# Two attentions in a diffusion trunk: a unit's transpose moved one unit back, scores of the differential heads read from 64 partitions

## The reference, cut to what matters

```python
def _attend(q, k, v, q2=None, k2=None, lam=None):
    scale = d ** -0.5
    def probs(qb, kk):
        s = jnp.einsum("bqhd,bkhd->bhqk", qb, kk) * scale
        return jax.nn.softmax(s, axis=-1)
    def one(qbs):
        p = probs(qbs[0], k)
        if q2 is not None:
            p = p - lam * probs(qbs[1], k2)
        return jnp.einsum("bhqk,bkhe->bqhe", p, v)

# B) latent attention: 8 heads, q and k of 96 channels, v of 64
# C) differential attention: 4 heads, q and k hold two maps of 64 channels each, v of 128
o_d = _attend(q_d[..., 0, :], k_all[..., 0, :], v_all, q_d[..., 1, :], k_all[..., 1, :], lam)
```

## Time and profile before

| | |
|---|---|
| three runs, median (lowest to highest) | 2794.98 us (2786.76 to 2797.15) |
| the profiled execution, own time | 2793.52 us |
| its span | 2791.7 us |
| TensorE matmul busy | 2615.9 us, 94% of the span |
| VectorE busy | 1334.8 us, 48% |
| ScalarE busy | 676.0 us, 24% |
| GpSimd busy | 1329.9 us, 48% |
| chain that ended last, TensorE's share | 82% |
| chain that ended last, VectorE's share | 10% |

### The profile page before, as it was taken

How to read it: one execution, slowest core, us unless ns; L and a number is a source line. 1 busy time by engine, 2 the same in 40 slices (tenths; PEclk the granted TensorE clock), 3 DMA queues, 4 the chain that set the end, 5 groups by cost and what they waited for, 6 DMA issues and landing times.

```text
span 2791.7 us, 41528 instructions
## 1 busy us (share of the span) xinstructions
PE 2615.9 (94%) x17328; PEld 2412.8 (86%) x17328; DVE 1334.8 (48%) x1693; ACT 676.0 (24%) x1202; POOL 1329.9 (48%) x604
## 2 busy tenths in 40 slices
PE   4999989999999799999979999899999988999997
PEld 3879986777999799999968799668789988999997
DVE  5434255777225644253644422649742266253353
ACT  2252235215311211010122423351343112010011
POOL 2524540340666466666644255205235655666663
PEclk8989999999999899999989999999999998999999
DMA  6201214430222122222211022242112211222221
GB/s 246 68 16 52 69 63 181 172 123 7 70 76 69 47 75 76 76 76 76 70 52 53 16 74 71 91 179 72 38 31 76 74 63 54 76 76 76 71 73 61
DMA packets 62555, 215.33 MB, mean 77 GB/s; under 512 B 6688, under 2 KB 11168, under 8 KB 62112
## 3 DMA queue, kind: packets, MB, share of 16 engines
q1 hardware_dynamic: 56448, 203.97, 21.6%
q10 hardware_dynamic: 5920, 8.70, 0.9%
HBM read 208.15 MB, written 4.49 MB: 76 GB/s over the span
## 4 chain that ended last, share of the span: by engine, by line
PE 82%; DVE 10%; ACT 2%; DVEq 2%; issue 1%; ACTq 1%; SPq 1%; DMA 1%
PE big L451 21%; PE big L455 21%; PE big L454 21%; PE big L606 4%; PE last_two L637 2%; PE two L620 2%; PE last_two L533 1%; PE big L474 1%; DVE cols L1342 1%; PE big L477 1%; PE two L751 1%; PE big L478 1%; PE last_two L751 1%; DVE ff_lo L1299 1%; DVE sq L1687 1%
## 5 line engine op out<-in xcount | busy, mean ns | idle before, releaser
L420 POOL TENSOR_TENSOR w_hi<-raw,cst 128x1024 fp32r<-128x1024 f32 x288 | 556.9, 1934 | 1335.2 <-PE big L451 1218.7
L451 PE MATMUL big<-act_hi,w_hi 128*128 128x320 f32 x2784 | 877.9, 315 | 43.9 <-DVE act_lo L1462 23.3
L454 PE MATMUL big<-act_lo,w_hi 128*128 128x320 f32 x2784 | 869.1, 312 | 0.0
L455 PE MATMUL big<-act_hi,w_lo 128*128 128x320 f32 x2784 | 868.8, 312 | 0.0
L423 POOL TENSOR_TENSOR w_lo<-raw,w_hi 128x1024 fp32r<-128x1024 f32 x288 | 742.3, 2577 | 41.0
L451 PEld LDWEIGHTS big<-act_hi,w_hi 128*128 128x128 f32 x2784 | 530.7, 191 | 61.1 <-issue 45.6
L454 PEld LDWEIGHTS big<-act_lo,w_hi 128*128 128x128 f32 x2784 | 531.1, 191 | 0.9
L455 PEld LDWEIGHTS big<-act_hi,w_lo 128*128 128x128 f32 x2784 | 530.6, 191 | 0.0
L451 PE MATMUL big<-ff_hi,w_hi 128*128 128x320 f32 x1024 | 317.6, 310 | 4.8 <-DVE ff_lo L1299 4.8
L455 PE MATMUL big<-ff_hi,w_lo 128*128 128x320 f32 x1024 | 316.4, 309 | 0.0
L454 PE MATMUL big<-ff_lo,w_hi 128*128 128x320 f32 x1024 | 316.4, 309 | 0.0
(11 more groups left out here) (295 smaller groups left out, 3491.5 us busy)
## 6 DMA issues: line engine op xcount, KB each, us to landing
raw<-in_w SPq DMA_DIRECT2D x368, 512.0 KB, 3.5
first_mod<-in_first SPq DMA_DIRECT2D x16, 512.0 KB, 19.0
x<-in_x ACTq DMA_DIRECT2D x1, 2560.0 KB, 12.9
out_y<-x SPq DMA_DIRECT2D x8, 320.0 KB, 2.3
cst<-in_const ACTq DMA_DIRECT2D x1, 1664.0 KB, 19.2
small<-in_small ACTq DMA_DIRECT2D x2, 437.0 KB, 9.1
out_C<-c_new ACTq DMA_DIRECT2D x2, 258.0 KB
v_d<-in_past ACTq DMA_DIRECT2D x2, 256.0 KB, 3.0
```

The source lines that it names most:

```text
L420: nc.gpsimd.tensor_tensor(w_hi[:, to, :], raw[:, slot, :], ones[:, 0:1].to_broadcast([P, BLK]), ALU.mult)
L451: first = mm(ps, wh, ah, start=k == 0, stop=False)
L454: mm(ps, wh, al, start=False, stop=False)
L455: last = mm(ps, wl, ah, start=False, stop=k == nk - 1)
```

## The change

- On TensorE, turn `i` now holds scores(i+1), turn(i-2), values(i-3); on ScalarE copyT(i-2); on VectorE the outputs come one turn later. The loops are one turn longer.
- There are four sets of probability tiles instead of three (the fourth set of `da` is `sq`, that of `ma` is `rs`) and four sets of columns for maxima and sums.
- In `da` the scores of map `m` read `q_d` and `k_d` at partitions 64m to 64m+63, and contract over 64 partitions. `q_map`, its clearing, `lay_out` and the semaphore `q_map_ready` are gone.
- The modulation beside `ma` moves one turn back in each of its steps: multiplications in turns 5 to 8 of each ten, the row kept in turn 9, turned and added in turn 10.

```diff
-            return prob[:, maps * (i % 3) + m, :] if i % 3 < 2 else (t1, rs)[m]
+            if i % 4 < 2:
+                return prob[:, maps * (i % 4) + m, :]
+            if maps == 1:
+                return (t1, rs)[i % 4 - 2]
+            return (t1, rs)[m] if i % 4 == 2 else sq[:, m, :]
...
-                    if p < 4 and 4 <= at < 8:
-                        if at == 4:
+                    if p < 4 and 5 <= at < 9:
+                        if at == 5:
...
-                    if p < 4 and at == 9:
-                        mod_turn(l, q, one[1][:, 256:512])
+                    if i >= 10 and at == 0:
+                        mod_turn(l, q - 1, one[1][:, 256:512])
...
-                    if maps == 2 and t == 0:
-                        pe.wait_ge(q_map_ready, l * H_D + h + 1)
...
-                for i in range(-1, n + 2):
+                for i in range(-1, n + 3):
                     if i + 1 < n:
                         scores(i + 1)
                     if beside and 0 <= i:
                         beside(i)
-                    if 0 <= i - 1 < n:
-                        turn(i - 1)
-                    if 0 <= i - 2 and (i - 2) % side == side - 1:
-                        if beside and i % 10 == 1:
-                            pe.wait_ge(mod_kept, l * MOD_CHUNKS + 3 + (i - 11) // 10)
-                        values((i - 2) // side)
+                    if 0 <= i - 2 < n:
+                        turn(i - 2)
+                    if 0 <= i - 3 and (i - 3) % side == side - 1:
+                        if beside and i % 10 == 2:
+                            pe.wait_ge(mod_kept, l * MOD_CHUNKS + 3 + (i - 12) // 10)
+                        values((i - 3) // side)
...
-                attend(l, "da", 2, 1, 40, 4, lambda h, m: q_map[h % 2][:, m, :], lambda h, m: k_d[:, h, :],
+                attend(l, "da", 2, 1, 40, 4, lambda h, m: q_d[64 * m:64 * m + 64, h, :],
+                       lambda h, m: k_d[64 * m:64 * m + 64, h, :],
...
-                    if i >= 3:
-                        act.wait_ge(pT_ready, l * 60 + unit0 + i - 2)
+                    if i >= 4:
+                        act.wait_ge(pT_ready, l * 60 + unit0 + i - 3)
...
-                for i in range(-1, n + 1):
-                    if i >= 1 and maps == 1:
-                        copyT(i - 1)
+                for i in range(-1, n + 2):
+                    if i >= 2 and maps == 1:
+                        copyT(i - 2)
                     if i + 1 < n:
                         exps(i + 1)
-                    if i >= 1 and maps == 2:
-                        copyT(i - 1)
+                    if i >= 2 and maps == 2:
+                        copyT(i - 2)
...
-                    if i % 10 == 8:
+                    if i % 10 == 9 and i < 40:
                         keep_row(l, 2 + i // 10, one[1][:, 256:512])
...
-                        if maps == 2 and t == LATE and h + 2 < heads:
-                            lay_out(h + 2)
                     if 0 <= i < n:
                         normalise(i)
-                    if i >= side + 2 and i % side == 0:
-                        outputs((i - side - 2) // side)
+                    if i >= side + 3 and (i - 1) % side == 0:
+                        outputs((i - side - 3) // side)
...
-                for tile in q_map:
-                    for m in range(2):
-                        other = 64 * (1 - m)
-                        v.memset(tile[other:other + 64, m, :], 0.0)
...
-                lay_out(0)
-                lay_out(1)
```

More of the change, by code:

```diff
@@ L219, in trunk @@
         qm, km = at("qm", [P, 2, T], A0), at("km", [P, 2, T], A0 + 5120)
-        q_map = [stage, sq]
         vm = at("vm", [P, 5, H_M, DV_1], A0 + 10240)
@@ L282, in trunk @@
         lam_tmp = cols[:, 9:12]
-        neg_max, row_sum = cols[:, 12:16], cols[:, 16:20]
+        neg_max, row_sum = cols[:, 12:20], cols[:, 20:28]
         raw_loaded = [sem(f"raw_loaded{i}") for i in range(RAW)]
@@ L294, in trunk @@
         cond_done = sem("cond_done")
-        q_map_ready = sem("q_map_ready")
         gather_done, small_sum = sem("gather_done"), sem("small_sum")
@@ L554, in hook @@
                                 pe.wait_ge(o_copied, l * 16 + 2 * p)
-                        for k in (2 * at - 8, 2 * at - 7):
+                        for k in (2 * at - 10, 2 * at - 9):
                             mod_block(l, KD * q + k, one[1][:, 256:512])
-                    if p < 4 and at == 9:
-                        mod_turn(l, q, one[1][:, 256:512])
+                    if i >= 10 and at == 0:
+                        mod_turn(l, q - 1, one[1][:, 256:512])
                 return hook
@@ L950, in exps @@
                         ps, b, _ = buf(use)
-                        col = 2 * (i % 2) + m
+                        col = 2 * (i % 4) + m
                         act.wait_ge(maxed, l * 80 + exp0 + maps * i + m + 1)
@@ L1329, in merge, with attend @@
                         behind(m)
-            def attend(l, name, maps, side, unit0, set0, heads, prob, exp0, out, lay_out=None, beside=None):
+            def attend(l, name, maps, side, unit0, set0, heads, prob, exp0, out, beside=None):
                 units = attention_units(heads, side)
@@ L1347, in normalise @@
                     n = CTX if t == LATE else T
-                    c0 = 2 * (i % 2)
+                    c0 = 2 * (i % 4)
                     dve.wait_ge(exped, l * 80 + exp0 + maps * (i + 1))
@@ L1371, in attend @@
                 n = len(units)
-                for i in range(-1, n + 3):
+                for i in range(-1, n + 4):
                     if i + 1 < n:
                         maxes(i + 1)
-                        h, t = units[i + 1]
-                        if maps == 2 and t == LATE and h + 2 < heads:
-                            lay_out(h + 2)
                     if 0 <= i < n:
                         normalise(i)
-                    if i >= side + 2 and i % side == 0:
-                        outputs((i - side - 2) // side)
+                    if i >= side + 3 and (i - 1) % side == 0:
+                        outputs((i - side - 3) // side)
                     if beside and i >= 0:
@@ L1431, in hook @@
                 def hook(i):
-                    if i % 10 == 9 and i < 40:
-                        q = 2 + i // 10
+                    if i % 10 == 0 and 10 <= i <= 40:
+                        q = 1 + i // 10
                         keep_mod(l, q, q, one[1][:, 256:512])
@@ L1671, in _ @@
                 dve.drain().then_inc(v_copied, 1)
-                attend(l, "ma", 1, 2, 0, 0, H_A, prob_a, 0, o_a, None, mods_beside(l))
+                attend(l, "ma", 1, 2, 0, 0, H_A, prob_a, 0, o_a, mods_beside(l))
                 for k in range(4):
@@ L1694, in _ @@
                         keep_mod(l + 1, 0, FIRST_CHUNKS[0], one[1][:, 0:256])
-                for tile in q_map:
-                    for m in range(2):
-                        other = 64 * (1 - m)
-                        v.memset(tile[other:other + 64, m, :], 0.0)
-                def lay_out(h):
-                    for m in range(2):
-                        r = slice(64 * m, 64 * m + 64)
-                        v.tensor_copy(q_map[h % 2][r, m, :], q_d[r, h, :])
-                    dve.drain().then_inc(q_map_ready, 1)
-                lay_out(0)
-                lay_out(1)
                 if l + 1 < DEPTH:
                     keep_mod(l + 1, 1, FIRST_CHUNKS[1], one[1][:, 0:256])
-                attend(l, "da", 2, 1, 40, 4, H_D, prob_d, 40, q_d, lay_out)
+                attend(l, "da", 2, 1, 40, 4, H_D, prob_d, 40, q_d)
                 for h in range(H_D):
```

## The result

The changed kernel takes **2809.7 us** (median of 7 runs, 2805.9 to 2815.3) against 2796.4 us (2786.8 to 2800.8) of the kernel before in the same session: ratio 1.0055, 95% interval 1.0036 to 1.0073. It is slower by about 13 us. The forecast was 2790 us and the range ended at 2804; both the sign and the range were wrong.

The account below looks back on a forecast made before the run. TensorE, busy 94% of the span, was taken as the bound, so its idle time and work count. Differential attention -2.1 us per layer twice, latent 0: -4 us from 2793.5 to 2789.5, stated as 2790 us; range 2775 to 2804.

Parts of the forecast that it names:

- The clearing and laying out: Differential attention: removing them gains nothing, being hidden by projections before it and gap-free scores within, except where VectorE is the bound.
- 64 partitions: Differential scores: a full unit takes 1.6 us by partial overlap of the maps, against 2.16; bounds 1.08 and 2.16.
- The prediction's own sign against it: Differential attention, full unit: scores over 2.1 us or under 1.3 would show the forecast wrong.
- The changes of mode: TensorE, differential attention: two changes between 64 and 128 partitions per unit, 0.2 us each; bounds zero and 0.2.
- A head: Differential attention: one head takes 17.5 us against 18.3, still waiting before the short unit's second map and the transposes after.
- the faster rival: Differential scores: both maps fully beside each other, mode changes free; -8 us per layer, about 2777 us; chance 0.10.
- The ends, first part: Start of the differential attention: the first five units take 16.3 us against 17.1.
- the rival on the clock: Differential attention: clock falls to half, two slow starts and one slow head cost +20 us; 2810 us; chance 0.07.
- The ends, last part: End of the differential attention: the last head, with the loop's extra turn, takes 22.1 us against 21.85.
- Both steps on the waits: Latent attention, per pair of heads: probabilities wait goes (-0.6 us), turned row's wait grows to 1.2 (+0.4); sum 0.
- The clause on the refill: Latent attention: modulation blocks read one unit later delay their slots' refill by about 2.5 us, costing nothing through GpSimd.
- The other rival: Differential scores: no overlap, 2.16 us per unit, mode changes paid; +3.3 us per layer, 2800 us; chance 0.18.

Follow-up runs that it names:

- scores128b: The change, but with 128-partition differential scores and q_map back, clearing and layouts in their old place; ratio 1.0022 to the kernel before.
- warm: The change plus unread filler multiplications before the first differential scores and after each of the first four units' scores; ratio 1.0025 to the kernel before.
- da_deep_warm: Kernel before with 64-partition scores, fillers and the deeper order in the differential attention alone; ratio 0.9993 to the kernel before.
- ma_deep_warm: Kernel before with 64-partition scores, fillers and the deeper order in the latent attention alone; 2791.5 us, ratio 0.9986 to the kernel before.
- only64_warm2: Repetition of only64_warm, the same kernel in another session; ratio 0.9976 to the kernel before.
- only64_warm: Kernel before with 64-partition differential scores in the old order, plus fillers at the start and after three units; ratio 0.9982 to the kernel before.

## Why the prediction was wrong

**The clearing and laying out:** nothing ahead of the attention, as said. In scores128b, which has both back, the stage's first scores come after the same 1.9 us of idle time as in the change, behind ScalarE's copy. What the layouts within the attention cost, no run shows apart.

**64 partitions:** the step gave 1.6 us for a full unit's scores. The traces have 1.28 with the change of mode. The eight records start in pairs 0.01 us apart, the pairs 0.27 us apart but for the first step and the step to the transposes, which take 0.1 more each. That is the lower bound of 1.08 and 0.2 for the change, both maps wholly beside each other although both multiplications of map 0 stand ahead of map 1's. The prediction's own sign against it, scores under 1.3, had come. The scores reach this only where both PSUM buffers are free. The Trainium skill (TensorEngine Tiling (Array Packing), Theoretical Speedup), held at arm's length in the prediction for want of such a row, had this right.

**The changes of mode** came to 0.4 us in a unit, as taken: 0.2 in the scores, 0.1 ahead of them (values 1.23 us, 677.80 to 679.03, against 1.12) and 0.07 in the transposes behind (0.61 against 0.54). The Trainium skill (TensorEngine Tiling (Array Packing), Key Properties) says that changing the tiling mode drains TensorE; these rows show what it cost here.

**A head:** 17.7 against 17.5, by the expected pattern of waits. Faster scores didn't shorten it further, because then the exponential that frees the second buffer is late. This also answers the faster rival: its overlap came, its time did not.

**The ends, first part: this is the first step that failed.** The sum had 16.3 us for the first five units at full clock (three ways round and the piece behind; "four" in its words is a slip); they took 21.4. The way round was right, 3.15 us for the first unit. What failed was the weight of the rival on the clock. I gave it 0.07, because the same start ran at full clock in layer 1 of before. But there TensorE works for 2.16 us of each 3.15. Here it works for 1.35, less even than the 1.6 of my own rival. That start was not the same. And layer 2 of before, whose stretches I called alike, had begun at half clock (0.57 in 1981.9 to 1985.9) and taken 77.4 us, not 75.5: the fall was there to be read, and only its length was new.

The rival's price per way round (1.07) was near the measured 1.18, and its time, 2810 us, is the measured one, partly by luck: no head ran at half clock for more than its first 1 to 2 us, and the latent part, which it left at zero, supplied the difference. The Trainium skill (TensorE: Matmul & The Clock Gate, The HAM clock gate) has the clock follow how busy TensorE was recently; the trace agrees. The experiment on it is warm: filling the idle time with work nobody needs makes the stage 4.7 us shorter. The sign set for this, a granted clock under 0.9 in the first layer's stage, had come with 0.85.

**The ends, last part: the second.** 22.1 us were forecast for the last head, 24.1 measured (679.03 to 703.09) and 23.3 in layer 2. From the short unit's first map on, the sum has 8.35 us and the traces 10.0 and 9.4; the 0.6 between the layers goes with the short drop of the clock in layer 1, and the rest with the copies that the transposes wait for. I had added up TensorE's work there and left no wait in it.

So the differential stage of 73.4 forecast came to 81.3: +5.1 at the start, +0.8 over two heads (the first took 18.1 us, the second 17.7), +2.0 at the end.

**The latent attention: the third.** Both steps on the waits were right in sign and near in size (1.04 us before the turned row, forecast 1.2). The clause on the refill was not: it asked only whether GpSimd, which takes the same places later, would wait, and not whether the modulation's own multiplications would. Their next blocks land in the places they have just released, and the move left 0.9 us less from release to use. This cost 2.9 and 4.5 us in the profile where nothing was forecast.

**The sum.** Differential +5.8 and +3.8, latent +3.7 and +4.8 in the profiles; of the 13 us between the medians about 8 are the clock (change against warm). What the deeper order costs lies between da_deep_warm, ma_deep_warm and only64_warm2: 4.4 and 2.8 us in the medians, where the intervals leave 4 to 5 us either way; what shows both costs is the stage lengths, not the time.

The kernel warm, which has both, is 13 us over only64_warm, of which its four stages show 7. In the profiles most of the rest lies where nothing was edited, between the first layer's differential and the second layer's latent attention: TensorE's 6719 instructions there take 1088.8 us in warm and 1082.5 in only64_warm, and in the 200 us in which they part, up to and in the second layer's mLSTM, the granted clock is 0.89 against 0.93. That stretch took 1085.3 to 1089.0 us in the six kernels with the deeper order in both attentions and 1082.4 to 1082.8 in the others, but 1088.3 in the profile of before. So it may be the change's doing or not; the runs leave it open.

**The other rival,** no overlap at 2800 us, was wrong in its reason: the scores ran side by side.

## What to carry to other kernels

When a change makes TensorE's work shorter in a stretch that is bound by a way round through other engines, work out its busy share there anew; the clock may take away more than the shorter work gives, and a few multiplications of no use can hold it. A deeper software pipeline pays at the end of every stage, so count its drain with its waits and not as work alone (9.4 us here against 7.1). Filling it cost nothing at full clock (first five units 17.2 us in warm, 17.6 in only64_warm2), but the slow clock lasted longer. And read such a start in every place where it occurs, not in the one that runs well. When the release of a buffer moves, list every reader of the next transfer into it, the moved one first.

## What the runs showed of the hardware

- Multiplications on opposite halves of the partitions ran wholly beside each other also when two of one half were issued before two of the other: 1.28 us with the change of mode for eight records of 320 columns, which took 2.16 on 128 partitions.
- In the change the granted clock went to 0.50 in the stage's first unit, with 1.35 us of work in 3.15 and no gap in TensorE's work above 1.90 us (2.12 in layer 2). It stayed there for 20 us, although its own slowness raised TensorE's busy time to 3.50 of each 4.33 us. It came back 7 to 9 us after the first transposes had joined in.
- Without fillers the clock fell at thirteen of fourteen starts of this stage, for 3 to 4 us with 128-partition scores and for 14 to 24 us with 64-partition scores; with fillers it fell at none of twelve.
- At 0.50 the scores of a unit took 3.50 us where the buffer wait allowed 2.34 at full clock.
